# A feed-forward's gate and up projections as seven block products instead of eight, and the next block's modulation computed in another stage

## The chip, the cores and the metric

The kernel runs on one core of a Trainium2 chip. The engines are named as the profile names them: PE (TensorE, with PEld for its weight loads), DVE (VectorE), ACT (ScalarE), POOL (GpSimd) and SP (SyncE, whose queue SPq issues the loads). The metric is the device time of one execution in microseconds; lower is better.

## What is computed

Two transformer blocks over one sequence of 1024 tokens with 1024 features, all in float32. The part that the change touches, from the reference (first block, `norm_ffn`, D_FF = 2816):

```python
merged = (jax.nn.sigmoid(g_a) * (y_a @ w_branch_a[i])
          + jax.nn.sigmoid(g_b) * (y_b @ w_branch_b[i]))
x = x + merged @ w_out[i]
h = rms_norm(x, norm_ffn[i])
x = x + (jax.nn.silu(h @ w_ffn_gate[i]) * (h @ w_ffn_up[i])) @ w_ffn_down[i]
...
# second block, before anything that depends on x
mod = jax.nn.silu(c) @ w_ada[l] + b_ada[l]
sh1, sc1, g1, sh2, sc2, g2 = jnp.split(mod, 6, axis=-1)
```

`c` is one vector of 1024, `w_ada` is 1024 x 6144 (25 MB), and `mod` is wanted only after the first block's end.

## The kernel before

Activations lie transposed, feature blocks of 128 on the partitions and the 1024 tokens along the row; KD = 8 blocks of input features, KF = 22 blocks of hidden features. A float32 product is made of three passes of the type `fp32r`: an operand is cut into a high part (rounded) and a low part (the rest), and PE adds high x high, high x low and low x high. So one 128 x 128 weight block against 1024 tokens is 3 parts x 2 halves of 512 tokens = 6 matmuls, and a unit of eight blocks (`project`, L545) is 48.

Weights go through three buffers of two halves each, `w_raw`, `w_hi` and `w_lo`. The loads stand in the order of `unit_list` (L206). For every unit SP loads `w_raw` (L3387), ACT copies it to `w_hi` (L1322), and POOL subtracts the two to `w_lo` (L3092); a copy waits until PE has done with the unit two before, a load until POOL has. PE writes `psum_mem`, eight banks of 512 columns used in pairs, whose order the class `Pairs` keeps. Every engine runs its instructions in program order, and semaphores tie them to each other.

The stages around the change, in the order of time:

- gating, about 350 to 630 us: for each of eight output blocks m PE makes the gate products `ga` and `gb` (48 matmuls each) and the branch products `ba` and `bb` (24 each, weights `w_branch_a` and `w_branch_b`). DVE scales the gates by the norm (L2150), multiplies by the branch products (L2381, L2387) and adds up `merged` (L2391). For m = 0 the pooled mixer's last steps stand before it (L2329 to L2353), and the lows `ya_lo` (L2310) between.
- out, about 636 to 715 us: `w_out` times `merged`, added to x (L2400; `x1` in the code, `x_block` in the profile), whose squares are summed for the norm.
- first feed-forward, about 715 to 1460 us: ACT and DVE make `h_hi` and `h_lo` (L1549, L2145). For i = 0 to 21 PE makes gate i and up i; the norm's factor is put on behind the product (L2150, L2450), ACT applies silu, DVE multiplies by up (L2453), and ACT and DVE cut the hidden block into `hid_hi_a` and `hid_lo_a` (L1587, L2467). Two hidden blocks make a group (FFN_GROUP = 2, N_GROUPS = 11); behind the gates and ups of group g comes the down projection of group g - 1, 8 output blocks x 2 hidden blocks x 6 = 96 matmuls, added to x by DVE, one addition per output block.
- In the same stage lies the modulation: 48 loads of 512 KB on SP, three per hidden block (`modulation_steps`), on DVE 48 multiply-adds over [128 x 1024] into `ada_sum` (L2419, L2422), and on PE six times eight column sums of one column each (L819) between a gate and an up.

The helper `unscale` is L2150, `inverse` the norm's factor on ACT (L1334) and DVE (L2122), `ahead` and `unit` the filling of the weight buffers on ACT, POOL and SP.

## Time and profile before

| what | value |
|---|---|
| time, median of 3 runs | 2874.87 us (2873.45 to 2876.5) |
| span of the profiled execution | 2872.1 us |
| PE busy | 2782.7 us, 12600 matmuls |
| PEld busy | 2223.4 us |
| DVE busy | 1319.2 us, 1464 instructions |
| ACT busy | 911.8 us, 1453 instructions |
| POOL busy | 812.1 us, 436 instructions |

The profiled execution spans 2872.1 us from its first to its last instruction; the runs' median is 2.8 us more. The page has busy times and the chain that ended last; the timeline names for an instruction with idle time before it, in brackets, the engine that ended this idle time. A PE duration in the timeline is from the start of a matmul to its modelled end and overlaps the next one's, so the pace of the stream is read from the spacing of the starts. The stage tables give for a stretch each engine's busy time with the count of instructions, and PEclk, the granted TensorE clock as a share of full speed.

### The profile page before, as it was taken

How to read it: one execution, taken by the hardware profiler on the slowest of the kernel's cores; microseconds unless marked ns; L12 is line 12 of the kernel's file. 1: busy time of each engine (PE TensorE's matmuls, PEld its weight loads, DVE VectorE, ACT ScalarE, POOL GpSimd, SP SyncE). 2: the span in 40 equal slices, each digit the busy share in tenths (PEclk: the TensorE clock that was granted, in tenths of full speed). 3: DMA queues.
4: the chain of work that ended last, by engine and by line, in shares of the span. 5: the costliest groups of instructions: out<-in, count | busy, mean ns of one | idle time of the engine just before them, and what ended most of it. 6: DMA issues, size and time to landing. Idle time of an engine off the chain costs nothing.

```text
span 2872.1 us, 30939 instructions
## 1 busy us (share of the span) xinstructions
PE 2782.7 (97%) x12600; PEld 2223.4 (77%) x12600; DVE 1319.2 (46%) x1464; ACT 911.8 (32%) x1453; POOL 812.1 (28%) x436
## 2 busy tenths in 40 slices
PE   8999999999999999999999999998989999999997
PEld 6666788887788888888877677887758888888885
DVE  6777842231434334343353646436273334444446
ACT  6666521122311111111154333355353212222223
POOL 2444522224122222222244221133432222222224
PEclk9999999999999999999999999999999999999998
DMA  3000011121123222221112102132221111111113
GB/s 116 23 23 23 17 50 48 47 104 56 66 100 113 88 88 88 107 77 58 53 44 98 67 31 49 31 81 77 104 82 54 49 52 45 44 52 44 51 45 132
DMA packets 65133, 184.98 MB, mean 64 GB/s; under 512 B 6616, under 2 KB 20184, under 8 KB 64864
## 3 DMA queue, kind: packets, MB, share of 16 engines
q1 hardware_dynamic: 64992, 183.01, 18.9%
q8 instruction: 100, 1.64, 0.2%
q14 instruction: 41, 0.34, 0.0%
HBM read 167.71 MB, written 15.27 MB: 64 GB/s over the span
## 4 chain that ended last, share of the span: by engine, by line
PE 85%; DVE 5%; issue 3%; ACT 3%; POOL 2%; DMA 1%; SPq 0%; POOLq 0%; DVEq 0%; ACTq 0%
PE psum_mem L559 64%; PE psum_mem L619 2%; PE psum_mem L955 2%; PE psum_mem L960 2%; PE psum_mem L957 2%; PE psum_mem L603 2%; PE psum_mem L654 1%; PE psum_mem L709 1%; POOL w_lo L3092 1%; PE psum_mem L657 1%; PE psum_mem L655 1%; PE psum_mem L1032 1%; PE psum_mem L1297 1%; PE psum_mem L997 1%; PE psum_mem L706 1%
## 5 line engine op out<-in xcount | busy, mean ns | idle before, releaser
L3092 POOL TENSOR_TENSOR w_lo<-w_raw,w_hi 128x1024 fp32r<-128x1024 f32 (+1 forms) x233 | 548.6, 2355 | 1742.4 <-ACT w_hi L1322 1742.4
L559 PE MATMUL psum_mem<-h_hi,w_hi 128*128 128x512 f32 x2096 | 654.4, 394 | 18.8 <-ACT h_hi L1355 9.2
L559 PE MATMUL psum_mem<-h_hi,w_lo 128*128 128x512 f32 x2096 | 650.2, 392 | 8.5 <-POOL w_lo L3092 8.5
L559 PE MATMUL psum_mem<-h_lo,w_hi 128*128 128x512 f32 x2096 | 649.6, 391 | 3.6 <-DVE h_lo L2914 2.7
L559 PEld LDWEIGHTS psum_mem<-h_hi,w_hi 128*128 128x128 f32 x2096 | 394.4, 189 | 107.6 <-ACT h_hi L1355 9.2
L559 PEld LDWEIGHTS psum_mem<-h_hi,w_lo 128*128 128x128 f32 x2096 | 394.8, 189 | 94.9 <-POOL w_lo L3092 12.6
L559 PEld LDWEIGHTS psum_mem<-h_lo,w_hi 128*128 128x128 f32 x2096 | 394.5, 189 | 89.6 <-DVE h_lo L2914 3.9
L1322 ACT CAST w_hi<-w_raw 128x1024 fp32r<-128x1024 f32 (+1 forms) x233 | 234.0, 1004 | 616.1 <-PE psum_mem L559 496.7
L2150 DVE TENSOR_TENSOR tmp_mem<-psum_mem,norm_row 128x1024 f32<-128x1024 f32 x44 | 53.9, 1224 | 280.8 <-PE psum_mem L559 280.8
L2475 DVE TENSOR_TENSOR x_block<-x_block,psum_mem 128x1024 f32<-128x1024 f32 x88 | 107.3, 1220 | 68.5 <-PE psum_mem L559 65.9
L3142 POOL TENSOR_TENSOR beta<-beta,left 128x128 f32<-128x128 f32 (+2 forms) x96 | 87.7, 915 | 141.0 <-DVE left L2266 139.0
L955 PE MATMUL psum_mem<-h_hi,w_hi 128*128 128x512 f32 x272 | 113.3, 417 | 4.9 <-POOL state L3270 3.8
L2050 ACT COPY ffn_conv_in<-psum_mem 128x1024 f32<-128x1024 f32 x44 | 44.7, 1016 | 214.1 <-PE psum_mem L559 214.1
L3033 DVE TENSOR_TENSOR y_mem<-y_mem,psum_mem 128x1024 f32<-128x1024 f32 x72 | 87.9, 1220 | 52.1 <-PE psum_mem L559 49.2
L559 PE MATMUL psum_mem<-hid_lo_a,w_hi 128*128 128x512 f32 x352 | 109.7, 393 | 0.0
L559 PE MATMUL psum_mem<-hid_hi_a,w_hi 128*128 128x512 f32 x352 | 109.3, 392 | 0.0
L559 PE MATMUL psum_mem<-hid_hi_a,w_lo 128*128 128x512 f32 x352 | 108.9, 390 | 0.0
L960 PE MATMUL psum_mem<-h_hi,w_lo 128*128 128x512 f32 x272 | 107.6, 395 | 0.0
L957 PE MATMUL psum_mem<-h_lo,w_hi 128*128 128x512 f32 x272 | 107.2, 394 | 0.0
L2453 DVE TENSOR_TENSOR tmp_mem<-tmp_mem,psum_mem 128x1024 f32<-128x1024 f32 x22 | 26.9, 1221 | 166.3 <-PE psum_mem L559 166.3
L559 PE MATMUL psum_mem<-hid_hi_b,w_lo 128*128 128x512 f32 x320 | 100.9, 397 | 0.0
L559 PE MATMUL psum_mem<-hid_lo_b,w_hi 128*128 128x512 f32 x320 | 100.7, 396 | 0.0
(382 smaller groups left out, 4137.9 us busy)
## 6 DMA issues: line engine op xcount, KB each, us to landing
ada_raw<-in_w_ada SPq DMA_DIRECT2D x48, 512.0 KB, 4.8
w_raw<-in_w_up_b SPq DMA_DIRECT2D x44, 512.0 KB, 3.3
w_raw<-in_w_in_a SPq DMA_DIRECT2D x32, 512.0 KB, 3.3
w_raw<-in_w_ffn_gate SPq DMA_DIRECT2D x22, 512.0 KB, 3.6
w_raw<-in_w_ffn_up SPq DMA_DIRECT2D x22, 512.0 KB, 3.3
w_raw<-in_w_ffn_down SPq DMA_DIRECT2D x22, 512.0 KB, 4.5
w_raw<-in_w_down_b SPq DMA_DIRECT2D x22, 512.0 KB, 3.3
w_raw<-in_w_in_b_ml SPq DMA_DIRECT2D x16, 512.0 KB, 3.4
```

The lines of the kernel that those rows point to most:

```text
L559: made = e.matmul(pairs.half(use, half), wt, x[:, half_of(half)], start=at == 0 and part == 0, stop=at == len(rhs) - 1 and part == 2, skip ...
L603: made = e.matmul(pairs.half(use, half), wt, x[:, cols], start=at == 0 and part == 0, stop=at == KD - 1 and part == 2, skip_group_check=True)
L619: return e.transpose(out, in_, ident)
L955: e.matmul(bank(6 + half), high, h_hi[:, k, cols], start=k == 0, stop=False, skip_group_check=True)
L957: e.matmul(bank(6 + half), high, h_lo[:, k, cols], start=False, stop=False, skip_group_check=True)
L960: made = e.matmul(bank(6 + half), low, h_hi[:, k, cols], start=False, stop=k == KD - 1, skip_group_check=True)
L1322: e.copy(w_hi[:, i, 0:width], w_raw[:, i, 0:width]).then_inc(*S.of("w_hi", c))
L2150: return e.tensor_tensor(out, ps, row[:, :], ALU.mult)
L2475: e.tensor_tensor(x1[:, m, :], x1[:, m, :], pairs.whole(("w_down", g - 1, m)), ALU.add).then_inc(*S.of("x1", (g - 1, m)))
L3033: e.tensor_tensor(y[:, m, :], y[:, m, :], pairs.whole(("w_down2", g - 1, m)), ALU.add).then_inc(*S.of("y_add", (g - 1, m)))
L3092: e.tensor_tensor(w_lo[:, i, 0:width], w_raw[:, i, 0:width], w_hi[:, i, 0:width].bitcast(F32), ALU.subtract).then_inc(*S.of("w_lo", c))
L3142: e.tensor_tensor(kept, kept, left[i % 3][:, HALF + 1 - width:HALF + 1], ALU.mult).then_inc(*S.of("weight", i))
```

## The change

**Seven products.** A gate block i and its up block i are taken as one product of 2 x 2 blocks. The weights are U (up) and G (gate), each cut in two along the input features (low: blocks 0 to 3, high: 4 to 7); the input X is cut along features and tokens into A (low features, tokens 0 to 511), B (low, 512 to 1023), C (high, 0 to 511) and E (high, 512 to 1023). Each of the seven products has 4 blocks x 3 parts of 512 tokens, 12 matmuls. By the names of the code:

| product | weights | operand ("form") |
|---|---|---|
| UP_LOW | U low | A |
| SUM_2 | G low + G high - U low | A + E - B |
| DIFF_3 | U low - G low | E - B |
| SUM_1 | -(G low + G high) | A - B |
| UP_HIGH | U high | C |
| GATE_HIGH | G high | C - A - E + B |
| DIFF_4 | U low + U high - G low - G high | E |

The operands are made once, between the out stage and pair 0: 28 blocks of [128 x 512], each with a high part by ACT and a low part by DVE. The weight sums are made anew for each pair on DVE: `weight_low_sum` (three steps) and `weight_high_sum` (one). `w_hi` and `w_lo` are filled in four slots of [128 x 512], seven copies by ACT and seven subtractions by POOL per pair. Three products are added up in other banks' results: ACT copies products 1 and 2 and the bank of product 4 to `parts` (`part`), DVE adds `parts` to the second product's bank (`b_sum`), and the gate comes out by `gate_read`. The order of the products is the table's; in pair 0 it is SUM_2 (three blocks), UP_LOW, DIFF_3 (three blocks), the last block of both, UP_HIGH, SUM_1, GATE_HIGH, DIFF_4. PSUM keeps three banks for even and three for odd pairs. A hidden block's norm, silu and up steps are now done in halves of 512 tokens (`gate_norm`, `gate_silu`, `gate_up`). Downs stand behind pairs 2, 4, ... 18 and the last two behind pair 21.

**Modulation.** It moves from the feed-forward to the gating stage, in blocks of half the width: 96 loads of 256 KB, on DVE 96 steps of [128 x 512] (14 per output block m until they are used up, in the places that `ADA_AFTER` gives), on PE twelve times four column sums before `ga`. `c_silu` is made by ACT in the attention stage. The first two loads wait for `u_centred` 3, the end of the pooling steps on DVE, and each further load for the step two before it. The loads of `p` go to a buffer of their own instead of `tmp`.

The core of the diff, in the order PE, ACT, DVE, SP:

```diff
+UP_LOW, SUM_2, DIFF_3, SUM_1, UP_HIGH, GATE_HIGH, DIFF_4 = range(7)
...
-        mod_step = {2 + (KD * part + KD - 1) // 3: part for part in range(6)}
+        N_ADA = 6 * NH
+        ADA_AFTER = (4, 5, 3, 2)
+        def mod_in(m):
+            return [q for q in range(N_ADA) if (KD * q + KD - 1) // sum(ADA_AFTER) == m - 1]
...
+        def w_slot(mem, slot):
+            return mem[:, slot // 2, half_of(slot % 2)]
+        def w_source(j):
+            if j in (SUM_1, SUM_2):
+                return w_sums[:, 0 if j == SUM_1 else 1, :]
+            return w_raw[:, 1 if j in (DIFF_3, GATE_HIGH) else 0, half_of(j not in (UP_LOW, DIFF_3))]
+        def gu_bank(i, j):
+            return bank(7 - 3 * (i % 2) - {UP_LOW: 0, UP_HIGH: 0, SUM_2: 1, SUM_1: 1, DIFF_4: 1, DIFF_3: 2, GATE_HIGH: 2}[j])
...
+                for q in mod_in(m):
+                    modulation(q)
                 one("w_ga", ("ga", m), h_rhs("a"), (("g_a", m),))
                 one("w_gb", ("gb", m), h_rhs("a"), (("g_b", m),))
...
+            def product(i, j, blocks=range(KH)):
+                for event in {UP_LOW: (("up", (i - 2, 0)),), SUM_2: (("up", (i - 2, 1)),), DIFF_3: (("gate", (i - 2, 0)),),
+                              UP_HIGH: (("part", (i, "low")),), SUM_1: (("part", (i, "two")),),
+                              GATE_HIGH: (("gate", (i, 1)),), DIFF_4: (("part", (i, "four")),)}[j]:
+                    if i >= 2 or j > DIFF_3:
+                        w.wait_ge(*event)
+                if i == 0 and j <= DIFF_3:
+                    w.wait_ge("x1", ("out", 4 if j == DIFF_3 else 5))
+                g = down_behind(i - 1)
+                if g is not None and j in (SUM_2, DIFF_3):
+                    w.wait_ge("x1", (g, KD - 2))
+                out, slot = gu_bank(i, j), j % 4
+                for k in blocks:
+                    high, low = (w_slot(mem, slot)[:, block_of(k)] for mem in (w_hi, w_lo))
+                    for part, (wt, x) in enumerate(((high, form_hi(j, k)), (high, form_lo(j, k)), (low, form_hi(j, k)))):
+                        w.wait_ge("form_lo" if part == 1 else "form_hi", (j, k))
+                        w.wait_ge("w_lo" if part == 2 else "w_hi", ("gu", i, j))
+                        made = e.matmul(out, wt, x, start=j <= DIFF_3 and k == 0 and part == 0,
+                                        stop=k == KH - 1 and part == 2, skip_group_check=True)
+                if blocks[-1] == KH - 1:
+                    made.then_inc(*S.of("full", ("gu", i, j)))
...
+                if 0 < i < KF - 1:
+                    hidden_high(i - 1)
+                w.wait_ge("full", ("gu", i, UP_LOW))
+                if i > 0:
+                    w.wait_ge("gate", (i - 1, 1))
+                else:
+                    w.wait_ge("form", (SUM_1, KH - 1))
+                part(i, "low", 0)
+                fill_pair(i, UP_HIGH)
+                fill_pair(i, GATE_HIGH)
+                w.wait_ge("b_sum", i)
+                if i > 0:
+                    w.wait_ge("gate", (i - 1, 0))
+                part(i, "two", 1)
+                if i == 0:
+                    for k in range(KH):
+                        form_high(SUM_1, k, form_raw[:, KH + k, :])
                     out_square(KD - 1)
...
+                    w.wait_ge("form", (GATE_HIGH, KH - 1))
+                    for k in range(KH):
+                        form_high(GATE_HIGH, k, form_raw[:, k, :])
...
+                fill_pair(i, DIFF_4)
+                if i == 0:
+                    for k in range(KH):
+                        form_high(DIFF_4, k, x1[:, KH + k, half_of(1)], vec("norm_ffn", KH + k))
+                w.wait_ge("full", ("gu", i, SUM_1))
+                part(i, "four", 0)
+                if i == 0:
+                    w.wait_ge("row_v", ("ffn", 7))
+                    inverse("ffn", norm_row, tmp[:, 1, :], [bank(half) for half in range(NH)])
+                gate_silu(i, 1)
+                if down_behind(i) is not None:
+                    for slot in range(4):
+                        fill_down(down_behind(i), slot)
+                        if slot == 1:
+                            gate_silu(i, 0)
+                elif i < KF - 1:
+                    fill_pair(i + 1, UP_LOW)
+                    fill_pair(i + 1, SUM_2)
+                    gate_silu(i, 0)
+                    fill_pair(i + 1, DIFF_3)
+                    fill_pair(i + 1, SUM_1)
...
+                modulation_some(ADA_AFTER[0])
                 for b, (name, use) in enumerate((("g_a", "ga"), ("g_b", "gb"))):
                     w.own(("by_a", "merged")[b])
                     w.wait_ge("full", (use, m))
                     unscale(tmp[:, b, :], pairs.whole((use, m))).then_inc(*S.of(name, m))
+                    if b == 0:
+                        for q in mod_in(m):
+                            take_modulation(q)
+                    modulation_some(ADA_AFTER[1 + b])
...
+            def weight_low_sum(i):
+                c = ff_unit["pair", i]
+                if i > 0:
+                    w.wait_ge("w_lo", ("gu", i - 1, SUM_1))
+                w.wait_ge("in_w1", c + 1)
+                w.own("w_sum")
+                e.scalar_tensor_tensor(out=w_source(SUM_1), in0=w_source(DIFF_3), scalar=-1.0, in1=w_source(GATE_HIGH),
+                                       op0=ALU.mult, op1=ALU.subtract).then_inc(*S.of("w_sum", (i, SUM_1)))
+                w.wait_ge("in_w0", c)
+                w.own("w_sum")
+                e.tensor_tensor(w_source(DIFF_3), w_source(UP_LOW), w_source(DIFF_3),
+                                ALU.subtract).then_inc(*S.of("w_sum", (i, DIFF_3)))
+                if i > 0:
+                    w.wait_ge("w_lo", ("gu", i - 1, SUM_2))
+                e.scalar_tensor_tensor(out=w_source(SUM_2), in0=w_source(UP_LOW), scalar=-1.0, in1=w_source(SUM_1),
+                                       op0=ALU.mult, op1=ALU.subtract).then_inc(*S.of("w_sum", (i, SUM_2)))
+            def weight_high_sum(i):
+                w.wait_ge("w_lo", ("gu", i, UP_HIGH))
+                w.own("w_sum")
+                e.tensor_tensor(w_source(DIFF_4), w_source(UP_HIGH), w_source(SUM_2),
+                                ALU.subtract).then_inc(*S.of("w_sum", (i, DIFF_4)))
...
+            def gate_read(i, half):
+                s = tmp[:, i % 2, half_of(half)]
+                w.wait_ge("part", (i, "four" if half else "two"))
+                w.wait_ge("full", ("gu", i, DIFF_3 if half else GATE_HIGH))
+                e.tensor_tensor(s, parts[:, 1 - half, :], gu_bank(i, DIFF_3), ALU.add).then_inc(*S.of("gate", (i, half)))
...
+                if 0 < i < KF - 1:
+                    hidden_low(i - 1)
+                b_sum(i)
+                if i == 0:
+                    for k in range(KH):
+                        form_low(SUM_1, k, form_raw[:, KH + k, :])
                     add_square("ffn", KD - 1, norm_row[:, :], tmp[:, (KD - 2) % 2, :])
...
+                    for k in range(KH):
+                        form_low(GATE_HIGH, k, form_raw[:, k, :])
+                weight_high_sum(i)
+                if i == 0:
+                    for k in range(KH):
+                        form_low(DIFF_4, k, x1[:, KH + k, half_of(1)], vec("norm_ffn", KH + k))
+                w.own("hid_lo")
+                gate_read(i, 1)
+                if i == 0:
+                    inverse("ffn", norm_row, tmp[:, 1, :], summed_in=[bank(half) for half in range(NH)])
+                    w.own("inv_v")
+                gate_norm(i, 1, "gate_normed")
+                if down_behind(i) is None and i < KF - 1:
+                    weight_low_sum(i + 1)
+                w.wait_ge("silu", (i, 1))
+                gate_norm(i, 1, "gate_scaled")
+                gate_read(i, 0)
+                gate_norm(i, 0, "gate_normed")
+                w.wait_ge("silu", (i, 0))
+                gate_norm(i, 0, "gate_scaled")
+                gate_up(i, 0)
+                gate_up(i, 1)
...
+                    if n >= 2:
+                        w.wait_ge("ada", ((n - 2) // KD, (n - 2) % KD))
+                    else:
+                        w.wait_ge("u_centred", 3)
+                    e.dma_start(ada_raw[n % 2][:, :], io["w_ada"][q // NH, k][:, half_of(q % NH)]).then_inc(
+                        *S.of(f"in_ada{n % 2}", n, 16))
+                    yield
+            modulation = modulation_steps()
+            for m in range(KD):
+                for n in ADA_AFTER:
+                    for _ in range(n):
+                        next(modulation, None)
+                    unit()
```

Line numbers of the changed kernel are higher by about 260 on DVE and 420 on SP, so L3387 before is L3794 after.

SP's queue from the end of the attention stage on, before (`in_w_in_a` are the gate weights here, `in_w_pool` the pooled mixer's):

```order
L3387 DMA w_raw<-in_w_in_a 128x1024 x2
L3387 DMA w_raw<-in_w_pool 128x128 x2
L3387 DMA w_raw<-in_w_branch_a 128x512
L3387 DMA w_raw<-in_w_branch_b 128x512
L3387 DMA w_raw<-in_w_in_a 128x1024 x2
L3387 DMA w_raw<-in_w_branch_a 128x512
L3387 DMA w_raw<-in_w_branch_b 128x512
L3387 DMA w_raw<-in_w_in_a 128x1024 x2
L3387 DMA w_raw<-in_w_branch_a 128x512
```

The same after:

```order
L3794 DMA w_raw<-in_w_in_a 128x1024 x2
L3794 DMA w_raw<-in_w_pool 128x128
L3822 DMA ada_raw<-in_w_ada 128x512 x4
L3794 DMA w_raw<-in_w_pool 128x128
L3822 DMA ada_raw<-in_w_ada 128x512 x5
L3794 DMA w_raw<-in_w_branch_a 128x512
L3822 DMA ada_raw<-in_w_ada 128x512 x3
L3794 DMA w_raw<-in_w_branch_b 128x512
L3822 DMA ada_raw<-in_w_ada 128x512 x2
L3794 DMA w_raw<-in_w_in_a 128x1024
L3822 DMA ada_raw<-in_w_ada 128x512 x4
L3794 DMA w_raw<-in_w_in_a 128x1024
```

Nine modulation loads now stand between the gate weights and `in_w_branch_a`, three before `in_w_branch_b`, and two, four and five before the following ones.

DVE's stream at the start of the gating stage, from the last pooling step (`u_centred` 3) on, before:

```order
L2344 TENSOR_TENSOR tmp_mem<-tmp_mem,u_mem 128x16
L2353 TENSOR_TENSOR pl_lo<-tmp_mem,pl_hi 128x1024
L2150 TENSOR_TENSOR tmp_mem<-psum_mem,norm_row 128x1024 x2
L2310 SCALAR_TENSOR_TENSOR ya_lo<-psum_mem,vecs,ya_hi 128x1024 x2
L2381 TENSOR_TENSOR merged<-tmp_mem,psum_mem 128x1024
L2387 TENSOR_TENSOR tmp_mem<-tmp_mem,psum_mem 128x1024
L2391 TENSOR_TENSOR merged<-merged,tmp_mem 128x1024
```

The same after (L2635 and L2638 are the modulation's sums, L2411 the scaling of a gate, L2571 `ya_lo`, L2677 and L2684 the two branch multiplications):

```order
L2605 TENSOR_TENSOR tmp_mem<-tmp_mem,u_mem 128x16
L2614 TENSOR_TENSOR pl_lo<-tmp_mem,pl_hi 128x1024
L2635 TENSOR_SCALAR ada_sum<-ada_raw,c_silu 128x512
L2638 SCALAR_TENSOR_TENSOR ada_sum<-ada_raw,c_silu,ada_sum 128x512 x3
L2411 TENSOR_TENSOR tmp_mem<-psum_mem,norm_row 128x1024
L2638 SCALAR_TENSOR_TENSOR ada_sum<-ada_raw,c_silu,ada_sum 128x512 x4
L2635 TENSOR_SCALAR ada_sum<-ada_raw,c_silu 128x512
L2411 TENSOR_TENSOR tmp_mem<-psum_mem,norm_row 128x1024
L2638 SCALAR_TENSOR_TENSOR ada_sum<-ada_raw,c_silu,ada_sum 128x512 x3
L2571 SCALAR_TENSOR_TENSOR ya_lo<-psum_mem,vecs,ya_hi 128x1024 x2
L2677 TENSOR_TENSOR merged<-tmp_mem,psum_mem 128x1024
L2638 SCALAR_TENSOR_TENSOR ada_sum<-ada_raw,c_silu,ada_sum 128x512 x2
```

Four, five, three and two sums stand before, between and behind the gate reads, and the two `ya_lo` are behind eleven of them.

DVE's stream at the start of the first feed-forward, before, from the last addition to x on:

```order
L2400 TENSOR_TENSOR x_block<-x_block,psum_mem 128x1024
L2145 SCALAR_TENSOR_TENSOR h_lo<-x_block,vecs,h_hi 128x1024 x3
L2141 TENSOR_TENSOR norm_row<-norm_row,tmp_mem 128x1024
L2145 SCALAR_TENSOR_TENSOR h_lo<-x_block,vecs,h_hi 128x1024 x5
L2126 SCALAR_TENSOR_TENSOR tmp_mem<-psum_mem,tmp_mem 128x512
L2129 SCALAR_TENSOR_TENSOR norm_row<-tmp_mem,norm_row 128x512
L2126 SCALAR_TENSOR_TENSOR tmp_mem<-psum_mem,tmp_mem 128x512
L2129 SCALAR_TENSOR_TENSOR norm_row<-tmp_mem,norm_row 128x512
L2150 TENSOR_TENSOR tmp_mem<-psum_mem,norm_row 128x1024
L2450 TENSOR_TENSOR tmp_mem<-tmp_mem,norm_row 128x1024
L2453 TENSOR_TENSOR tmp_mem<-tmp_mem,psum_mem 128x1024
```

The same after (L2722 and L2724 make the lows of forms, L2783 is `b_sum`, L2402 a square's addition, L2715 the high weight sum, L2790 `gate_read`, L2387 the first step of the norm's factor):

```order
L2722 TENSOR_TENSOR form_lo<-form_raw,form_hi 128x512
L2724 SCALAR_TENSOR_TENSOR h_lo<-x_block,vecs,h_hi 128x512 x4
L2752 SCALAR_TENSOR_TENSOR form_raw<-x_block,vecs,form_raw 128x512
L2746 SCALAR_TENSOR_TENSOR form_raw<-x_block,vecs,parts 128x512
L2783 TENSOR_TENSOR psum_mem<-psum_mem,parts 128x512
L2722 TENSOR_TENSOR h_lo<-form_raw,h_hi 128x512 x4
L2402 TENSOR_TENSOR norm_row<-norm_row,tmp_mem 128x1024
L2722 TENSOR_TENSOR h_lo<-form_raw,h_hi 128x512 x4
L2715 TENSOR_TENSOR w_raw<-w_raw,w_sums 128x512
L2724 SCALAR_TENSOR_TENSOR h_lo<-x_block,vecs,h_hi 128x512 x4
L2790 TENSOR_TENSOR tmp_mem<-parts,psum_mem 128x512
L2387 SCALAR_TENSOR_TENSOR tmp_mem<-psum_mem,tmp_mem 128x512
```

The first `gate_read` stands behind twelve lows, a square's addition and a weight sum, all of which follow the first `b_sum`.

## Rows read from the trace of the kernel before

**Rows 1.** The page, its part 1 and its part 4 by engine.

```profile
PE 2782.7 (97%) x12600; PEld 2223.4 (77%) x12600; DVE 1319.2 (46%) x1464; ACT 911.8 (32%) x1453; POOL 812.1 (28%) x436
...
PE 85%; DVE 5%; issue 3%; ACT 3%; POOL 2%; DMA 1%; SPq 0%; POOLq 0%; DVEq 0%; ACTq 0%
```

**Rows 2.** Stretches: PE, PEld, DVE, ACT, POOL busy us (count); PEclk, DMA share, GB/s.

```profile
400.00:440.00 40.00, 40.00 (x177) 32.81 (x176) 9.45 (x6) 6.25 (x8) 8.12 (x5) 1.00 0.14 42
762.00:1455.00 693.00, 692.91 (x3090) 572.30 (x3089) 272.58 (x229) 119.27 (x117) 160.06 (x66) 1.00 0.24 85
```

**Rows 3.** Timeline of PE: start, duration, engine, line, what, idle before and releaser.

```profile
764.63 0.62 PE L559 MATMUL psum_mem<-h_hi,w_hi 128*128 128x512 f32 x2
...
799.99 0.62 PE L559 MATMUL psum_mem<-h_hi,w_hi 128*128 128x512 f32 x2
...
1700.21 0.39 PE L957 MATMUL psum_mem<-h_lo,w_hi 128*128 128x512 f32 x1
...
1702.71 0.39 PE L955 MATMUL psum_mem<-h_hi,w_hi 128*128 128x512 f32 x1
...
2826.34 0.40 PE L1297 MATMUL psum_mem<-hid_lo_b,w_hi 128*128 128x512 f32 x1
...
2829.85 0.39 PE L1297 MATMUL psum_mem<-hid_lo_b,w_hi 128*128 128x512 f32 x1
```

**Rows 4.** Groups by form: busy us, mean ns of one (last row: 760 to 1455 us).

```profile
L3092 POOL TENSOR_TENSOR w_lo<-w_raw,w_hi 128x512 fp32r<-128x512 f32 x16 | 20.7, 1296 | 127.5 <-ACT w_hi L1322 127.5
L2971 DVE SCALAR_TENSOR_TENSOR h_lo<-tmp_mem,mod,h_hi 128x512 fp32r<-128x512 f32 x16 | 12.0, 748 | 1.8 <-ACT h_hi L2003 1.4
L1322 ACT CAST w_hi<-w_raw 128x512 fp32r<-128x512 f32 x16 | 9.9, 620 | 130.2 <-PE psum_mem L559 130.2
...
L2467 DVE TENSOR_TENSOR hid_lo_a<-tmp_mem,hid_hi_a 128x1024 fp32r<-128x1024 f32 x21 | 25.6, 1220 | 3.3 <-ACT hid_hi_a L1587 3.3
```

**Rows 5.** DMA issues: count, size of one, median us from issue to landing.

```profile
w_raw<-in_w_ffn_up SPq DMA_DIRECT2D x22, 512.0 KB, 3.3
...
w_raw<-in_w_branch_a SPq DMA_DIRECT2D x8, 256.0 KB, 2.6
```

**Rows 6.** Timelines of DVE, SPq and PE, gating stage.

```profile
375.65 0.18 DVE L2344 TENSOR_TENSOR tmp_mem<-tmp_mem,u_mem 128x16 f32<-128x16 f32 x1
...
378.56 0.33 SPq L3387 DMA_DIRECT2D w_raw<-in_w_branch_a  x1
...
383.14 0.63 PE L559 MATMUL psum_mem<-ya_hi,w_hi 128*128 128x512 f32 x2
...
394.64 0.39 PE L559 MATMUL psum_mem<-h_hi,w_hi 128*128 128x512 f32 x1
...
428.92 3.33 DVE L2391 TENSOR_TENSOR merged<-merged,tmp_mem 128x1024 f32<-128x1024 f32 x1
...
461.92 3.33 DVE L2391 TENSOR_TENSOR merged<-merged,tmp_mem 128x1024 f32<-128x1024 f32 x1
```

**Rows 7.** Timelines of PE and ACT, start of the first feed-forward.

```profile
716.62 0.70 PE L559 MATMUL psum_mem<-h_hi,w_hi 128*128 128x512 f32 x2 [1.28 <-DVE x_block L2400]
...
741.28 1.04 PE L559 MATMUL psum_mem<-h_hi,w_hi 128*128 128x512 f32 x2
...
753.44 0.70 PE L559 MATMUL psum_mem<-h_hi,w_hi 128*128 128x512 f32 x2 [0.66 <-ACT w_hi L1322]
...
755.90 0.73 PE L559 MATMUL psum_mem<-h_hi,w_lo 128*128 128x512 f32 x2 [1.30 <-POOL w_lo L3092]
...
737.20 1.28 ACT L1329 ACT_TABLE_LOAD   x1
```

**Rows 8.** Timeline of POOL, gating stage.

```profile
461.79 2.39 POOL L3092 TENSOR_TENSOR w_lo<-w_raw,w_hi 128x1024 fp32r<-128x1024 f32 x1 [3.20 <-ACT w_hi L1322]
```

**Rows 9.** Timeline of PE and the table of stretches, second block.

```profile
1909.26 0.80 PE L955 MATMUL psum_mem<-h_hi,w_hi 128*128 128x512 f32 x1 [3.76 <-POOL state L3270]
...
1910.00:1919.00 9.00, 9.00 (x47) 7.73 (x46) 2.67 (x7) 3.62 (x15) 6.12 (x6) 0.76 0.31 82
```

642 lines of the change are left out of this document (431 added, 211 removed).

## The prediction

> **What bounds the kernel now.** I read the page first: TensorE (PE) is busy 97% of the span and carries 85% of the chain that ended last; the other engines are below half [rows 1]. The table by stretches then says where this matters. From 762 to 1455 us, nearly the whole first feed-forward, PE is busy 692.91 of 693.00 us at full granted clock, with DVE at 39%, POOL at 23%, ACT at 17%; a stretch of the gating stage is as full, DVE at 24%, POOL at 20% [rows 2]. So only fewer matmuls shorten either stage, and anything added costs only where PE starts to wait. The PE timeline gives the price of one: between the two rows of the gate and up stream lie 156 matmuls in 35.36 us, 0.2267 us each. The new code uses each weight block for one matmul of 512 columns, not two; a stream of that form is there already, eleven matmuls from 1700.21 to 1702.71 us, 0.2273 us each [rows 3]. I take 0.2267.
>
> **A. Fewer matmuls.** A pair (gate and up block i) was 2 x 8 x 3 x 2 = 96 matmuls and is 7 x 4 x 3 = 84, hence 22 x 12 = 264 fewer: **-59.8 us**. The down projection keeps its 96 per group, and the modulation's one-column matmuls (96 rows) only move: 0.
>
> **B. Does a steady pair stay at PE's pace?** A pair is now 84 x 0.2267 = 19.04 us, a product 2.72. Durations of the new 512-wide steps, from their nearest rows: ACT copy 0.62, DVE 0.75, POOL low half 1.30 [rows 4]. Per pair that is DVE 13 x 0.75 + 1.22 = 11.0 us, POOL 7 x 1.30 = 9.1, ACT 12 x 0.62 and one of at most twice that = 8.7: none is a bound. The waits, in order, from the end of pair i: DVE's last multiply ends 1.6 us in, then ACT's hidden high part (1.2), its copy of the first product (0.62), DVE's hidden low part (1.22), until 4.7 us. The second product ends at 5.44; add on DVE, copy on ACT: 6.9 us. The fourth product may start at 8.16: 1.2 us to spare. Later: copy of the fourth product, then DVE's read, ready 1.5 us after it, before the sixth product at 2.72: again 1.2. Weights for the next pair: a raw half leaves after POOL's last low half, lands 3.3 us later [rows 5], and is split 2 to 3 us before use. I cost the steady pairs at **0**; if this cover goes, rival 2 has the price. In the down groups DVE has 2.75 us per block for one addition of 1.22, and the three weight sums (2.2 us) stand behind the fourth: late by less than one block, 0.
>
> **C. Modulation in the gating stage, first block.** The order printed above puts the nine first modulation loads ahead of `w_branch_a` on SP, all behind the last pool step on DVE, at 375.83 us; before, that load left at 378.56 [rows 6]. There are two buffers, so two loads go per round of load (2.6, the row of the same size, rows 5), sum (0.75) and the signals: 3.5 us. Loads 0 and 1 land at 378.6, sums 2 and 3 end at 383.4, then the gate read (1.2), sums 6 and 7 at 390; load 8, then `w_branch_a` leaves at 390.0, lands at 392.6, is cast 0.6 and subtracted 1.3 later. PE wanted it at 383.14 [rows 6]. DVE also makes `ya_lo` 2 and 3 behind sum 11, at 400.6, which that product needs for its last two blocks. Branch b then ends at 407.3, against 394.6 before, where the next block's first matmul starts [rows 6]: **+12.7**.
>
> **D. The other blocks.** A block took 33.0 us: the additions at 428.92 and 461.92 [rows 6]. Fourteen sums are seven rounds, 25 us, but broken by the four reads. Worst is `w_branch_b`: it leaves after sum 9, which stands behind the second gate read, at 24.6 us into the block, lands with its neighbour's traffic at 27.9, is cast at 28.6 and has its low half at 30.0; PE wants it at 27.6 and 28.5. I take 1.5 us for each of six blocks (the next block's cast is late by less), **+9**. The bounds are 0 (load alone at 2.6, a little PE time from the moved matmuls) and 3.5 (every load of the block late).
>
> **E. The first pair.** Before, pair 1 began 26.0 us after the start and lost 0.66 + 1.30 in its second unit [rows 7]. Now DVE forms 4 x 7 operand blocks and their low halves. Counted from the end of the last out block, T (715.3, one wait of 1.28 ahead of the row at 716.62): DVE reaches the last forms at T+13.5, because 4 lows, and form 4 and 1 of block 3, stand ahead of the copy the fifth product waits for; that product's weights are there at T+16, PE having run out at T+10. Sixth product: its bank is freed by a read that stands on DVE behind 4 + 1 + 4 + 1 + 4 steps (order above), T+30, PE having run out at T+21. Then the sum, ACT's two table loads (1.28 each, rows 7) and six inverse steps of half a row (0.62) stand ahead of the weight cast of pair 1: T+41, PE having run out at T+36.4. Pair 1 is effectively under way at T+42.6 and loses 0.9 more at its fourth product. Before, the same point was at 26.0 + 1.96 = T+28.0; with the 2.7 us that A already books, **+18**. Bounds: 8 (half of these waits overlap) and 28 (POOL's halves come in between, next paragraph).
>
> What POOL can do to DVE a row shows: DVE's `merged` started at 461.92 beside POOL's `w_lo` of 461.79 to 464.18 and took 3.33 us, where the same form beside nothing takes 1.22 [rows 4, 6, 8]. The Trainium skill, SBUF — State Buffer, Who interferes with whom, says that a DVE instruction with two SBUF inputs and a GpSimd instruction that reads SBUF exclude each other for a whole instruction, and the trace agrees. By that rule every weight sum, norm multiplication and low half here competes with POOL; that is rival 2.
>
> **F. The clock.** Around a PE wait of 3.76 us the granted clock is 0.76 over 9 us: 0.24 x 9 = 2.2 us lost against full speed, the mean of a stretch at 2.4 GHz and one at the lower level, 1.2 GHz [rows 9]. C and E bring four waits of 4 us and more: 4 x 2.2 = **+9**; bounds 0 and 15. The Trainium skill, TensorE: Matmul & The Clock Gate, What's actually happening, says the gate passes half the pulses after idleness; the row agrees.
>
> **Sum.** -59.8 + 12.7 + 9 + 18 + 9 = -11. The end of the stage keeps its steps in their order (last additions, squares, sum): 0. The profiled execution spans 2872.1 us, the runs' median is 2874.87, 2.8 more: 2861 of span, **2864 us**.
>
> **The rivals.** (1) *The starts hide better*: C at 7, D 0, E 8, F 2, a gain of 43, **2832 us**. For: ACT and DVE have over half their time free in both stages; my chains add every step end to end. Against: the SP and DVE orders are strict. (2) *DVE and POOL block each other in every pair* (slower): POOL holds 9.1 us of a pair, DVE's eight steps with two SBUF inputs and the hidden low part 6.8, together 15.9 of 19.04. If two halves of 1.3 us fall into the chain of B, 2.6 less the 1.2 to spare is 1.4 us per pair, 21 pairs: +29, **2893 us**. It decides the sign from 11 / 21 = 0.5 us per pair. For: that load. Against: POOL's halves in B fall mostly where DVE waits for PE, and all DVE steps on a PSUM bank (the b sum, reads, up) have one SBUF input and no row shows them held up. (3) *The new stream is slower*: at the 0.234 us per matmul of the last down block (15 from 2826.34 to 2829.85, rows 3), 22 x 84 x 0.0073 adds 13 us: **2877 us**, no change. Against: the rows at 1700.21 and 1702.71, whose operands are `h_hi` as here. (4) *The change doesn't act*, the stage being bound by weight loads: 2875 or more; PE's full windows and PEld at 83% speak against it, I give it nothing.
>
> **How the numbers follow.** Measurement tells about 0.2%, 5.7 us, so "faster" is below 2869. Forecast 0.50 (0.39 faster, 0.09 same, 0.02 slower, as its bounds lie), rival 1 0.25, rival 2 0.14, rival 3 0.11 (0.01 faster, 0.06 same, 0.04 slower). Faster 0.65, same 0.15, slower 0.20. The range runs from just past rival 1 to just short of rival 2: 2828 to 2888.
>
> **What would show it.** Right: the pair matmuls' count down by 264 at 0.227 us; PE full from pair 2 on, about 627 us for the stage without its start; PE waits before `w_branch_a` near 384 us (about 9 us) and before every `w_branch_b`; in the first pair waits for DVE's `tmp_mem` read and ACT's `w_hi`; several short dips of the clock. Wrong: PE gaps in each pair before the fourth or sixth product, released by DVE or POOL (rival 2); no gap at `w_branch_a` (C false).

## The result and the profile after

The changed kernel takes **2899.76 us** (median of 4 runs, 2897.57 to 2906.73) against 2875.68 for the kernel before in the same comparison (4 runs): a ratio of 1.0088 with a 95% interval of 1.0071 to 1.0105. It is slower by 24 us, where 2864 with a range of 2828 to 2888 was predicted. The profiled execution spans 2895.8 us, 23.7 more than the one before. Times are medians of all runs; in the comparisons below one run of the kernel before and one of the third-buffer kernel took over 4500 us, and the ratios leave such slow runs out.

The page, its part 1 and its part 4 by engine, which answer to [rows 1]:

```profile
PE 2758.6 (95%) x12336; PEld 2185.1 (75%) x12336; DVE 1499.7 (52%) x1774; ACT 1015.9 (35%) x1698; POOL 925.9 (32%) x568
...
PE 79%; DVE 7%; issue 6%; ACT 3%; POOL 3%; DMA 2%; SPq 0%; DVEq 0%; POOLq 0%; ACTq 0%
```

The 264 matmuls are gone (12600 to 12336), but PE's share fell from 97% to 95%: PE stands idle 48 us longer than before (137.2 us against 89.4). The table of stretches of the changed kernel says where. It shows the end of gating block 0, the blocks 1, 2, 3 and 6 and the steady part of the feed-forward (columns as in [rows 2]):

```profile
378.00:412.00 34.00, 22.45 (x78) 16.87 (x77) 19.81 (x20) 8.44 (x11) 6.73 (x5) 0.75 0.44 142
412.00:448.00 36.00, 34.84 (x155) 27.76 (x154) 12.04 (x15) 4.22 (x5) 4.97 (x3) 1.00 0.36 117
448.00:495.00 47.00, 38.61 (x160) 30.64 (x159) 20.62 (x24) 6.32 (x7) 8.26 (x5) 0.85 0.40 134
495.00:536.00 41.00, 37.40 (x161) 29.63 (x160) 20.23 (x23) 5.26 (x6) 7.73 (x5) 0.96 0.44 141
...
608.00:654.00 46.00, 37.76 (x165) 30.12 (x164) 20.70 (x25) 6.41 (x8) 9.93 (x5) 0.89 0.45 141
...
824.00:1430.00 606.00, 606.00 (x2620) 491.76 (x2619) 323.69 (x362) 190.23 (x307) 252.90 (x183) 1.00 0.16 53
```

The steady feed-forward is full, as forecast. The gating blocks 1 to 7, 33.0 us each before, are not alike: 35.9, 47.3, 41.0, 36.2, 35.4, 45.8 and 34.8 us, and block 0 ends 18 us late. By the starts of the PE rows the stages compare so:

| stage | before, us | after, us | difference |
|---|---|---|---|
| up to the end of gating block 0 | 394.40 | 412.12 | +17.7 |
| gating blocks 1 to 7 | 231.0 | 276.3 | +45.3 |
| out stage | 89.9 | 88.9 | -1.0 |
| first feed-forward, to the sum of its squares | 753.8 | 719.2 | -34.5 |
| the rest | 1403.0 | 1399.2 | -3.8 |

The last row is the second block, which the change leaves as it was; the profiles of the other kernels with the same second block have 1403 to 1406 us there, and why this one has 1399 is not known. So the feed-forward gave 34.5 us and the gating stage took 63.0. PE's longest waits, summed over the run (the page of waits: engine and line, releaser, us in total, times, longest):

```profile
PE psum_mem L652 <- ACT w_hi L1482: 30.2, 12, 7.9
PE psum_mem L652 <- POOL w_lo L3479: 10.3, 10, 1.5
...
PE psum_mem L936 <- ACT w_hi L1711: 7.7, 2, 3.9
PE psum_mem L964 <- DVE x_block L2816: 7.2, 4, 4.3
PE psum_mem L936 <- DVE tmp_mem L2790: 6.0, 1, 6.0
```

Of the first line 29.3 us, in 11 waits, lie in the gating stage. What ends such a wait, at the start of block 2, is seen when the timelines of DVE, SPq and PE are laid side by side:

```profile
436.92 0.74 DVE L2638 SCALAR_TENSOR_TENSOR ada_sum<-ada_raw,c_silu,ada_sum 128x512 f32<-128x512 f32 x1
449.05 0.49 DVE L2635 TENSOR_SCALAR ada_sum<-ada_raw,c_silu 128x512 f32<-128x512 f32 x1 [11.40 <-PE psum_mem L881]
...
438.11 0.38 SPq L3794 DMA_DIRECT2D w_raw<-in_w_branch_b  x1
449.57 1.18 SPq L3822 DMA_DIRECT2D ada_raw<-in_w_ada  x2
450.85 0.38 SPq L3794 DMA_DIRECT2D w_raw<-in_w_in_a  x1
...
448.00 1.84 PE L881 MATMUL psum_mem<-consts,ada_sum 128*128 128x1 f32 x16
456.73 1.19 PE L652 MATMUL psum_mem<-h_hi,w_hi 128*128 128x512 f32 x2 [6.89 <-ACT w_hi L1482]
```

A modulation unit is one of the twelve blocks of 512 columns, numbered from 0. DVE is through with unit 2 at 437.7 and stands **11.40 us**, because unit 3 writes the same one of the two `ada_sum` buffers as unit 1, and PE makes unit 1's column sums only at the start of the next block (L881, 448.00). SP's next modulation loads wait for DVE's sums, and behind them in its queue stands the gate weight of block 2 (L3794 at 450.85). It leaves 2.9 us after PE began the block that needs it. The label on PE's wait is ACT, four links behind the cause. The same happens where unit 10 begins, at block 6: DVE stands 11.42 us and PE then waits 6.87.

### The profile page after: what moved, and what is told of

It is laid out like the page before. It is cut to its first block, busy times and chain, and to the rows that moved or that the text cites. A ratio compares the mean times of both kernels' runs of the same rounds, so it can differ in the third digit from the quotient of the medians.

```text
span 2895.8 us, 31514 instructions
## 1 busy us (share of the span) xinstructions
PE 2758.6 (95%) x12336; PEld 2185.1 (75%) x12336; DVE 1499.7 (52%) x1774; ACT 1015.9 (35%) x1698; POOL 925.9 (32%) x568
## 4 chain that ended last, share of the span: by engine, by line
PE 79%; DVE 7%; issue 6%; ACT 3%; POOL 3%; DMA 2%; SPq 0%; DVEq 0%; POOLq 0%; ACTq 0%
PE psum_mem L652 36%; PE psum_mem L936 14%; PE psum_mem L964 8%; PE psum_mem L712 2%; PE psum_mem L1115 2%; PE psum_mem L1120 2%; PE psum_mem L1117 2%; POOL w_lo L3479 2%; PE psum_mem L696 1%; PE psum_mem L747 1%; PE psum_mem L802 1%; PE psum_mem L750 1%; PE psum_mem L748 1%; DMA ada_raw<-in_w_ada 1%; PE psum_mem L1192 1%
## 5 line engine op out<-in xcount | busy, mean ns | idle before, releaser
L3479 POOL TENSOR_TENSOR w_lo<-w_raw,w_hi 128x1024 fp32r<-128x1024 f32 (+2 forms) x167 | 386.8, 2316 | 1232.1 <-ACT w_hi L1482 1219.5
L652 PE MATMUL psum_mem<-h_hi,w_hi 128*128 128x512 f32 x1392 | 440.0, 398 | 29.4 <-ACT w_hi L1482 16.0
L652 PE MATMUL psum_mem<-h_hi,w_lo 128*128 128x512 f32 x1392 | 434.9, 394 | 9.1 <-POOL w_lo L3479 9.1
L652 PEld LDWEIGHTS psum_mem<-h_hi,w_hi 128*128 128x128 f32 x1392 | 263.7, 191 | 90.1 <-DVE tmp_mem L2684 13.9
L1482 ACT CAST w_hi<-w_raw 128x1024 fp32r<-128x1024 f32 (+2 forms) x167 | 165.2, 989 | 450.3 <-PE psum_mem L652 194.7
L652 PEld LDWEIGHTS psum_mem<-h_hi,w_lo 128*128 128x128 f32 x1392 | 263.3, 190 | 69.5 <-POOL w_lo L3479 14.7
L652 PEld LDWEIGHTS psum_mem<-h_lo,w_hi 128*128 128x128 f32 x1392 | 264.9, 191 | 61.3 <-DVE h_lo L3301 3.6
L3571 POOL TENSOR_TENSOR w_lo<-w_raw,w_hi 128x512 fp32r<-128x512 f32 x154 | 216.6, 1410 | 294.4 <-ACT w_hi L1711 294.2
L2816 DVE TENSOR_TENSOR x_block<-x_block,psum_mem 128x1024 f32<-128x1024 f32 x88 | 107.4, 1221 | 101.6 <-PE psum_mem L964 101.4
L1711 ACT CAST w_hi<-w_raw 128x512 fp32r<-128x512 f32 x154 | 94.7, 622 | 167.0 <-PE psum_mem L936 81.9
L936 PE MATMUL psum_mem<-h_hi,w_lo 128*128 128x512 f32 x352 | 138.8, 394 | 0.1
L936 PE MATMUL psum_mem<-form_hi,w_hi 128*128 128x512 f32 x264 | 105.6, 400 | 3.7 <-ACT w_hi L1711 3.7
L1120 PE MATMUL psum_mem<-h_hi,w_lo 128*128 128x512 f32 x272 | 107.4, 395 | 0.0
L936 PE MATMUL psum_mem<-form_hi,w_lo 128*128 128x512 f32 x264 | 105.7, 401 | 1.5 <-POOL w_lo L3571 1.5
```

The costliest lines, as they stand in the source:

```text
L652: made = e.matmul(pairs.half(use, half), wt, x[:, half_of(half)], start=at == 0 and part == 0, stop=at == len(rhs) - 1 and part == 2, skip ...
L936: made = e.matmul(out, wt, x, start=j <= DIFF_3 and k == 0 and part == 0, stop=k == KH - 1 and part == 2, skip_group_check=True)
L1120: made = e.matmul(bank(6 + half), low, h_hi[:, k, cols], start=False, stop=k == KD - 1, skip_group_check=True)
L1482: e.copy(w_hi[:, i, 0:width], w_raw[:, i, 0:width]).then_inc(*S.of("w_hi", c))
L1711: e.copy(w_slot(w_hi, slot), source).then_inc(*S.of("w_hi", key))
L2816: e.tensor_tensor(x1[:, m, :], x1[:, m, :], down_banks(g, m), ALU.add).then_inc(*S.of("x1", (g, m)))
```

## The experiments

Every comparison is with the kernel before, run on the same chip in between (its medians were 2876.1 to 2876.8 us). A number in the text that is not a median comes from the profile of that run.

### The modulation left out, after and before

In both kernels the loads of `w_ada`, the weighted sums and the column sums are left out, so `mod` is only `b_ada`. The core of the edit, in the changed kernel:

```diff
-                for q in mod_in(m):
-                    modulation(q)
...
-                w.wait_ge("full", ("mod", q))
-                e.tensor_tensor(mod[:, cols], pairs.whole(("mod", q))[:, 0:KH], vec("b_ada", q * KH, KH),
-                                ALU.add).then_inc(*S.of("mod", q))
+                e.tensor_scalar(mod[:, cols], vec("b_ada", q * KH, KH), 1.0, None, ALU.mult).then_inc(*S.of("mod", q))
```

> The changed kernel with the modulation left out: no loads of w_ada, no weighted sums, no column sums; mod is only b_ada. Theory 1 (the loss lies in how the modulation is interleaved with the gating stage): the gating stage falls back from 318 us to about 255 us, the time to about 2836 (2899.8 less 63). Rival (the seven products themselves are no gain, the gating stage is slow for another reason, such as the three new halves' pace): 2875 or more.

> The kernel before with the modulation left out in the same way. Its 96 column sums take 0.106 us each in the trace, so both theories expect 2875.7 - 10 = 2865. The difference to after_no_mod is what the seven products alone are worth: 29 us by theory 1 (59.8 less the first pair 17, the end 7 and a slower pace 8), under 10 us by the rival. If it were 2850 or less, the modulation had cost more than its column sums before, too.

Measured: 2844.02 us after (ratio 0.9876, 0.9861 to 0.9890) and 2866.48 before (0.9958, 0.9943 to 0.9973). The gating blocks are 33.0 us each in both. The kernel after is 8 us above the 2836 that theory 1 expected. So the seven products alone are worth 22.5 us, not 29, and the modulation costs 55.7 us in the changed kernel and 9.8 in the one before. The last number is about its column sums: 96 rows of 0.106 us each in the trace, 10.2 us. The loss is in the interleaving, as theory 1 has it; the seven products are a gain, though 7 us smaller than stated.

### A third buffer for the weighted sums

```diff
+        third_sum = merged[:, KD - 1, HALF:T]
+        sums = [ada_sum[0][:, :], ada_sum[1][:, :], third_sum]
...
-                            if q > 1:
-                                w.wait_ge("full", ("mod", q - 2))
+                            if q > 2:
+                                w.wait_ge("full", ("mod", q - 3))
```

> The changed kernel with a third buffer for the weighted sums (it lies in the last row of merged, unused until block 7), so that the first sum of unit q waits for the column sums of q - 3, not q - 2. Theory 1a (the long waits come from DVE standing 11.4 us for column sums that PE has only at the start of the next block, with the weight loads queued behind): the two waits of 6.9 us at blocks 2 and 6 and the 1.4 + 1.2 of block 3 go, with their clock loss 25 to 33 us: 2868 to 2875. Rival 1b (the weight loads are late because they stand behind the modulation's loads on SP, two buffers being too few for them, whatever DVE waits for): the waits stay, less than 8 us is gained.

Measured: 2877.92 us (0.9998, 0.9986 to 1.0010), 21.8 less than the change and just above the 2868 to 2875 expected. The gating stage ends 27.3 us earlier (661.15 instead of 688.43). Of that, 2.4 arose in block 0, where the edit does not act yet; 24.9 are blocks 1 to 7, which all take 35 to 36.5 us, and the timeline of DVE and SPq at the same place reads:

```profile
435.12 0.48 DVE L2637 TENSOR_SCALAR ada_sum<-ada_raw,c_silu 128x512 f32<-128x512 f32 x1
...
439.27 0.38 SPq L3796 DMA_DIRECT2D w_raw<-in_w_in_a  x1
```

DVE goes on without a wait and the gate weight leaves at 439.27, 6 us ahead of block 2. Both 6.9 us waits and the two at the start of block 3 are gone. Rival 1b (two load buffers are too few, whatever DVE waits for) is out: their number was not touched. The total gained 5.5 us less than the stage; in the two profiles the second block, the same in both kernels, took 1404.8 us here and 1399.2 with the change.

### The weight loads ahead of the modulation loads

```diff
                 for n in ADA_AFTER:
+                    unit()
                     for _ in range(n):
                         next(modulation, None)
-                    unit()
```

> The changed kernel with only SP's order turned round: in each place the weight load first, then the modulation loads. DVE still stands for the column sums. Theory 1a and 1b both expect the waits for w_hi to go, since no weight load is behind a modulation load of its own place: first block 17.7 to about 5 us of loss, blocks 2 and 6 from 14 to about 4 each, 30 to 40 us gained in all: 2860 to 2870. If DVE's wait holds PE up by itself (reads of the gates and branches late, banks not free), less than 20 us is gained.

Measured: 2878.25 us (1.0005, 0.9995 to 1.0014), 21.5 less than the change, where both theories expected 30 to 40: at the edge of the case in which DVE's wait holds PE up by itself. Blocks 3, 4 and 7 now take 34.8 us and blocks 1 and 5 33.9, which is 33.0 and two or one sets of column sums (0.85 us each): nothing else is left of the modulation there. Blocks 2 and 6 take 39.2 and 39.6, with this row at the start of block 2:

```profile
450.91 1.22 PE L652 MATMUL psum_mem<-h_hi,w_hi 128*128 128x512 f32 x2 [1.74 <-DVE merged L2677]
```

PE waits for a bank that DVE, still standing for the column sums, reads late. The wait is only 1.74 us, but the granted clock is 0.50 around it (451 to 455 us), and the slower matmuls cost 2.8 more. And the first block is no better than before the edit (+19.0 us), with another label:

```profile
402.84 1.22 PE L652 MATMUL psum_mem<-ya_lo,w_hi 128*128 128x512 f32 x2 [13.79 <-DVE ya_lo L2571]
```

There the twelve sums that stand ahead of `ya_lo` on DVE hold PE up by themselves, and the late weight mattered little beside them. Term C of the prediction had both paths, and its end, 407.3, was reckoned from `ya_lo`; the expectation of this run (17.7 to about 5 us) had left that path out.

### The gating stage mended

The third buffer, the loads first, and no sum ahead of the first block's gate reads and `ya_lo`:

```diff
+        def ada_after(m):
+            return (0, 0, 6, 8) if m == 0 else ADA_AFTER
...
-                    modulation_some(ADA_AFTER[1 + b])
-                if m == 0:
-                    map_low(2)
-                    map_low(3)
+                    if m == 0 and b == 1:
+                        map_low(2)
+                        map_low(3)
+                    modulation_some(ada_after(m)[1 + b])
```

> The changed kernel with the third buffer for the sums, the weight loads ahead of the modulation loads on SP, and in the first block no sum ahead of the gate reads and ya_lo (0, 0, 6, 8 instead of 4, 5, 3, 2). If theory 1a is whole, nothing but the column sums (0.106 us each, 10 us in all) is left of the modulation in this stage: gating 266 to 272 us instead of 318, out stage from 2 us behind 625.4 + 10, the time 2844 + 10 = 2854 to 2862. If DMA traffic or DVE's and POOL's sharing cost by themselves, blocks stay above 34.5 us each and the time above 2868.

Measured: 2862.76 us (0.9953, 0.9938 to 0.9968), just above what was expected, and 0.5% less than the kernel before. The stage ends 23.4 us behind that of before, not 63.0. Two of its blocks in the table of stretches:

```profile
475.80:510.60 34.80, 34.80 (x161) 28.80 (x160) 20.28 (x22) 5.46 (x6) 7.50 (x4) 1.00 0.48 151
510.60:545.40 34.80, 34.80 (x162) 28.82 (x161) 18.96 (x22) 5.47 (x6) 6.86 (x4) 1.00 0.44 145
```

DVE is busy 20 of 35 us and the DMA moves over three times what it did in [rows 2], and PE waits for nothing in them. Neither the traffic nor the sharing between DVE and POOL costs anything here. What stays is a wait of 5.9 us ahead of block 1's column sums, for the eighth sum, since none starts before the lows. Block 1 then takes 38.1 us, its first 6 at a granted clock near 0.50, and block 2 36.3, with one wait of 1.2 us for `w_lo`.

### Thirty-two bytes of padding

The prediction gave 0.11 to a slower stream (rival 3), and the timeline of the changed kernel shows it: pairs 3 and 4 with the down group between them and the next pair.

```profile
883.42 0.39 PE L936 MATMUL psum_mem<-form_hi,w_hi 128*128 128x512 f32 x1
...
922.06 0.63 PE L964 MATMUL psum_mem<-hid_hi_a,w_hi 128*128 128x512 f32 x2
...
944.46 0.39 PE L936 MATMUL psum_mem<-form_hi,w_hi 128*128 128x512 f32 x1
```

Two pairs take 38.64 us, 0.2300 per matmul, and a down group 22.40, 0.2333 (before 21.99). Within a pair the three products on `form_*` go at 0.2333, the four on `h_*` at 0.2267. Before the change too, matmuls on `ya_*`, `yb_*` and `hid_*_b` were at 0.2333. The buffers of the fast kind begin, in each partition, at the same address modulo 256 as the weights: `w_hi` begins at byte 28384 and `h_hi` at 57056, both 224 modulo 256, but `form_hi` at 155392 and `hid_hi_a` at 204544, both 0, which is 32 off. In the kernel before `hid_hi_a` was 64 off and `hid_hi_b` 96. Two kernels add unused bytes:

```diff
         eps_col = sb("eps_col", [P, 2])
+        sb("pad", [P, 8])
```

> The changed kernel with 32 unused bytes per partition behind the buffers that live all through (a pad of 8 floats). Before it, weights and h_hi/h_lo begin at an address 32 past a multiple of 64 in each partition, and form_hi, form_lo, hid_*_a, ya, yb at a multiple of 64; the pad moves the second kind to 32 past, like the first. In the trace matmuls on h_* start 0.2267 us apart, on form_* and hid_* 0.2333. Theory 2 (the pace hangs on where the streamed operand lies): form_* and hid_*_a fall to 0.2267, a pair from 19.32 to 19.04 us, a down group from 22.40 to 21.76, the feed-forward by 6 + 7 = 13 us, ya and yb by 2.6, and hid_*_b too, 6: 2899.8 - 20 = 2880. Rival (the pace belongs to something else of these streams, such as one bank per weight load or the halves' readers): no change, 2900.

> The kernel before with the same 32 bytes ahead of the weight buffers: now weights, h_* and hid_*_a lie at multiples of 64, ya, yb, hid_*_b at 32 past. Theory 2a (what counts is the streamed operand's own address): h_* slows down to 0.2333, ya, yb and hid_*_b come to 0.2267; 7000 matmuls x 0.0067 = 47 us more and some 8 us less: 2915. Theory 2b (what counts is that operand and weights lie alike): h_* stays at 0.2267, yb and hid_*_b (32 against 0) stay at 0.2333: 2876. Rival (no address matters): every pace as before.

Measured for the pad behind the common buffers: 2895.90 us (1.0065, 1.0048 to 1.0081), 3.9 less than the change; the feed-forward is 7.3 us shorter, the second block, 1404.4 us in this profile, 5.2 longer. The same places:

```profile
884.33 0.39 PE L937 MATMUL psum_mem<-form_hi,w_hi 128*128 128x512 f32 x1
...
922.69 0.63 PE L965 MATMUL psum_mem<-hid_hi_a,w_hi 128*128 128x512 f32 x2
...
944.68 0.39 PE L937 MATMUL psum_mem<-form_hi,w_hi 128*128 128x512 f32 x1
```

38.36 and 21.99: `form_*` and `hid_*_a`, now 64 off, go at 0.229, two thirds of the way. `hid_*_b`, now 128 off, stayed at 0.2334. So the address counts, but the expected 0.2267 was wrong. With the pad ahead of the weights in the kernel before the time was 2876.41 (1.0000, 0.9990 to 1.0011): this pad moves the weights and every buffer behind them by 32 bytes, so that their addresses change and no distance between them does. `h_*` kept 0.2267 and `yb_*` 0.2333. That rejects 2a (the operand's own address) and leaves the distance between operand and weights.

### Pair 0 in another order

The edit orders the small steps of pair 0 as the expectation says; in its core, on DVE:

```diff
                 weight_high_sum(i)
-                if i == 0:
-                    for k in range(KH):
-                        form_low(DIFF_4, k, x1[:, KH + k, half_of(1)], vec("norm_ffn", KH + k))
                 w.own("hid_lo")
                 gate_read(i, 1)
                 if i == 0:
+                    for k in range(KH):
+                        form_low(DIFF_4, k, x1[:, KH + k, half_of(1)], vec("norm_ffn", KH + k))
+                    gate_read(0, 0)
+                    weight_low_sum(1)
                     inverse("ffn", norm_row, tmp[:, 1, :], summed_in=[bank(half) for half in range(NH)])
```

> The changed kernel with pair 0 alone in another order: ACT fills UP_HIGH's and GATE_HIGH's weights ahead of its first copy, DVE makes the first gate_read ahead of DIFF_4's lows and the second ahead of the norm's factor, PE sums the squares ahead of GATE_HIGH, pair 1's first two weight slots are filled before and amid ACT's steps for the factor, hidden block 0 is cut after pair 1's b_sum. Theory 3 (the 15 us of waits in the first pair are the order of the small steps, nothing else): the wait of 6.0 us for the read and that of 3.8 for w_hi all but go, pair 1 starts 28 to 31 us after the stage's start instead of 40.7, and may lose up to 3 us in its middle: 8 to 12 us less, 2888 to 2892. Rival (ACT and DVE are simply full there, so any order moves the wait): under 3 us gained.

Measured: 2892.54 us (1.0058, 1.0041 to 1.0075), 7.2 less than the change and just short of the 8 to 12 expected; the feed-forward is 9.1 us shorter. The changed kernel's waits in the first pair were

```profile
790.57 0.77 PE L936 MATMUL psum_mem<-h_hi,w_hi 128*128 128x512 f32 x1 [3.95 <-ACT w_hi L1711]
...
804.84 0.79 PE L936 MATMUL psum_mem<-h_hi,w_hi 128*128 128x512 f32 x1 [6.04 <-DVE tmp_mem L2790]
...
818.03 0.50 PE L936 MATMUL psum_mem<-form_hi,w_hi 128*128 128x512 f32 x1 [3.75 <-ACT w_hi L1711]
819.98 0.79 PE L936 MATMUL psum_mem<-form_hi,w_lo 128*128 128x512 f32 x1 [1.22 <-POOL w_lo L3571]
```

and in the reordered one

```profile
794.22 0.79 PE L936 MATMUL psum_mem<-h_hi,w_hi 128*128 128x512 f32 x1 [5.32 <-ACT parts L1776]
...
804.73 0.50 PE L936 MATMUL psum_mem<-h_hi,w_hi 128*128 128x512 f32 x1 [0.69 <-DVE tmp_mem L2801]
```

The wait for the read fell from 6.04 to 0.69 and pair 1 starts at 810.3, 30.7 us into the stage instead of 40.7. That of 3.75 for `w_hi` fell to 1.60, but 1.4 us in two waits for `w_lo` came in pair 1. The first wait did not go: SUM_1 cannot start before ACT's copy, which DVE's last form releases. As I read it, that is the amount of work between the out stage and pair 0 and not its order; no run here took it apart. The rival (any order only moves the wait, under 3 us gained) is out.

### All together

Gating mended, pair 0 reordered, two hidden lows behind the first additions of a down group, and 224 unused bytes ahead of `form_hi`:

```diff
+        sb_in(ff1, "pad", [P, 56])
         form_hi_mem = sb_in(ff1, "form_hi", [P, 3, KH, HALF], F32R)
...
-            for i in range(HID_LAST, KF):
-                hidden_low(i)
             for m in range(KD):
                 down_add(N_GROUPS - 2, m)
+                if m in (1, 2):
+                    hidden_low(HID_LAST + m - 1)
```

> Gating mended (2862.8 measured), pair 0 reordered, the last two hidden lows behind the first additions of down group 9, and 224 unused bytes ahead of form_hi, so that form_* and hid_*_a lie at the same offset within 256 bytes as the weights and h_*. If the pace of a stream hangs on that offset, a pair comes from 19.32 to 19.04 us and a down group from 22.40 to 21.76 or less, 13 us; if 64 bytes are what counts, 19.18 and 21.99 as with the pad of 32, 7 us. Sum: 2862.8 - 10 (first pair) - 2 (end) - 7 to 13: 2838 to 2844, faster than both kernels by over 1%. Rival: the gains overlap (the stage's end or the DVE steps take them back) and it stays above 2852.

Measured: **2841.39 us** (0.9884, 0.9868 to 0.9901). The pace, at the pairs of the same kind:

```profile
893.80 0.39 PE L942 MATMUL psum_mem<-form_hi,w_hi 128*128 128x512 f32 x1
...
931.88 0.62 PE L970 MATMUL psum_mem<-hid_hi_a,w_hi 128*128 128x512 f32 x2
...
953.64 0.39 PE L942 MATMUL psum_mem<-form_hi,w_hi 128*128 128x512 f32 x1
```

Two pairs 38.08 and a down group 21.76, both exactly 0.2267 per matmul. The two hidden lows were worth little: one wait of 1.2 us at the stage's end went, the one of 4.3 stayed. The section on the prediction shows what that one hangs on.

The last two kernels carry the addresses through: the kernel before with nothing but unused bytes, and the mended one with the same bytes for the second block.

```diff
+            sb_in(ff, "pad_b", [P, 40])
             hid_hi_b = [sb_in(ff, f"hid_hi_b{i}", [P, FFN_GROUP, T], F32R) for i in range(2)]
```

> The kernel before with nothing but unused bytes: ahead of p_*, of hid_*_a and of hid_*_b, so that all three lie at the same offset within 256 bytes as the weights. Theory 2c (a matmul starts 0.2267 us after the last where streamed operand and weights lie alike within 256 bytes, 0.229 where they differ by 64, 0.2334 otherwise): the second block's down groups from 22.4 to 21.8 us, 1056 x 0.0067 = 7 us, the first block's from 21.99 to 21.76, 2.5 us: 2876.5 - 9.5 = 2867. Rival (it holds for the form_* stream only): 2874 or more.

> all_mended (2841.4) with the same bytes ahead of p_*, hid_*_last and hid_*_b, and in the first block's gating 0, 2, 6, 6 sums instead of 0, 0, 6, 8, so that the first column sums don't wait. Theory 2c: 7 to 8 us less in the second block; the wait of 5.4 us at block 1 falls to 2 or less and its clock loss with it, 3 to 5 us: 2829 to 2832. Rival: above 2838.

Measured: 2866.46 us (0.9961, 0.9949 to 0.9972) for the kernel before with the bytes, 10.2 less for no instruction changed, and **2833.66 us** (0.9849, 0.9836 to 0.9862) for the best version, 43 less than the kernel before. A down group of the second block in the former:

```profile
2535.36 0.61 PE L562 MATMUL psum_mem<-hid_hi_b,w_hi 128*128 128x512 f32 x2
...
2557.12 0.62 PE L562 MATMUL psum_mem<-h_hi,w_hi 128*128 128x512 f32 x2
```

21.76 us, where the kernel before has 22.41:

```profile
2537.95 0.63 PE L559 MATMUL psum_mem<-hid_hi_b,w_hi 128*128 128x512 f32 x2
...
2560.36 0.63 PE L559 MATMUL psum_mem<-h_hi,w_hi 128*128 128x512 f32 x2
```

The other edit of the best version, 0, 2, 6, 6 sums in block 0, missed: the wait fell from 5.4 to 3.1 us, but the gating stage ended at 648.3 as in the version ahead of it.

## Why the prediction was wrong

**A** held: 264 matmuls fewer, and at the pace of `h_*` 59.8 us. **B** held too: from 824 to 1430 us PE is busy 606.00 of 606.00 us, and rival 2 (DVE and POOL block each other) did not come, although POOL's half-width step took 1.41 us on average with 42% load. The time lies near rival 2's 2893, but not for its reason.

**D was the step that failed.** It priced the blocks behind the first at 9 us (1.5 for each of six, with a bound of 3.5), and blocks 1 to 7 took 45.3: 22.3 of waits, 10.2 of column sums and 12.8 more, most of them slower matmuls (see F). The step that it called the worst, `w_branch_b`, cost less than it said: six waits of 0.6 to 0.9 us, 4.4 in all. The one that it dismissed, "the next block's cast is late by less", cost 6.89 us at block 2 and 6.87 at block 6. The term walked through DVE's sums and SP's loads block by block and asked when each load leaves. It did not ask what the sums themselves wait for. The kernel's line on the wait for the column sums of q - 2 is in the part that moved, and in the feed-forward it never bound. With two buffers, 8 sums per unit and 14 per block, units 3, 5 and 10 begin before PE has reached the column sums that they need, and DVE stands 11.40, 6.54 and 11.42 us there, 29.4 in all. The run with the third buffer shows what that is worth: 24.9 us in these blocks. The 10.2 us of column sums moved here from the feed-forward, where they went out of the sum again: the 0 for them was right.

**C** was forecast as +12.7 and was +16.3 (17.7, of which 1.4 arose ahead of the stage). Both waits that it named came, for `w_branch_a` and for `ya_lo`:

```profile
395.36 1.19 PE L652 MATMUL psum_mem<-ya_hi,w_hi 128*128 128x512 f32 x2 [7.91 <-ACT w_hi L1482]
...
402.54 0.98 PE L652 MATMUL psum_mem<-ya_lo,w_hi 128*128 128x512 f32 x2 [1.83 <-DVE ya_lo L2571]
```

The predicted 9 us wait before `w_branch_a` was 7.91. One of 1.81 us for the second pool weight, behind four modulation loads, was not foreseen, and 4.8 us of the 16.3 are matmuls at the lower clock.

**E** was right in its end: pair 1 under way 42.6 us after the start was forecast, 41.9 measured (818.03, 1.22 more, less 777.35), with the waits for `w_hi`, the read and `w_hi` at their places. They were shorter than forecast (3.95, 6.04 and 3.75 us for about 6, 9 and 5), and the 0.9 us more at its fourth product did not come. The slower matmuls between these waits are in the 41.9.

**F** was mis-sized and in the wrong place. It gave four waits 2.2 us each, three of them in the first pair. In the gating stage PE's waits sum to 33.8 us, the column sums to 10.2, 1.4 came from ahead, and 63.0 less these leaves 17.6 us. Of these, 14.9 lie in blocks 0, 2, 3 and 6, where the granted clock is 0.75, 0.85, 0.96 and 0.89, and are put down to matmuls at the lower clock; the other 2.7 are spread over blocks whose clock is 1.00, and their cause is open. The blocks with a wait of about 7 us lost 3.0 and 4.3 more than their waits, and with the loads first the blocks with one of 1.7 us, right behind the column sums, lost 2.8 and 3.1 more.

**The end of the stage**, costed at 0 because its steps keep their order, took 7.2 us in four waits for DVE's additions (L2816). The last down groups follow pair 21 at once, and on DVE the lows of its hidden blocks stand ahead of the additions: that is the wait of 1.21. Two in the last group, 0.30 and 1.37, were not looked into. The one of 4.33 hangs on another step that moved, the low part of `p`:

```profile
1442.57 0.62 ACT L1711 CAST w_hi<-w_raw 128x512 fp32r<-128x512 f32 x1 [6.39 <-PE psum_mem L964]
1443.10 1.99 ACT L1850 CAST p_hi<-p_raw 128x1024 fp32r<-128x1024 f32 x2
...
1444.17 1.51 DVE L2862 TENSOR_TENSOR p_lo<-p_raw,p_hi 128x1024 fp32r<-128x1024 f32 x1 [6.22 <-ACT p_hi L1850]
...
1446.87 0.85 PE L964 MATMUL psum_mem<-hid_hi_a,w_hi 128*128 128x512 f32 x2 [4.33 <-DVE x_block L2816]
```

ACT makes `p_hi` behind a weight copy that waits for PE, DVE makes `p_lo` ahead of its third addition, and PE waits for that addition. Before, `p_lo` was made ahead of the last two groups' additions (L2462). No run here takes this apart; that the wait stayed at 4.33 when the hidden lows were moved fits it.

**The pace** (rival 3, 13 us at 0.234 in all seven products) was half right: three of seven products go at 0.2333, 5.6 us, and the down groups, which it left out, add 4.5. The row at 2826.34 that it came from was an instance of the same effect, and "whose operands are `h_hi` as here" overlooked that three products read `form_*`.

In all: -59.8, then +63.0 for the gating stage less the 10.2 of column sums that the feed-forward gave up, +16.6 for the first pair (13.9 and the 2.7 that A books), +7.2 and +10.1 give +26.9; the out stage and the rest were 4.8 us shorter, which gives 22.1, and the span is 23.7 longer. The 1.6 left over was not taken apart in full: beyond their pace and their waits, pairs 1 and 2 took 3.1 us more (the first pairs before 1.0) and the last two down groups 2.6, while a wait before the sum of the squares fell from 2.52 to 0.88.

## What to carry to other kernels

When work is moved to another place, list every wait of the moved code again, those that never bound included, and for each ask where the releasing step now stands in its own engine's order; the two buffers of the weighted sums never held anything up in the feed-forward and became a stall where PE took the sums only at the start of a block. On a queue that issues in order, as SP's does here, put the loads that the bound engine needs ahead of those that serve side work, since everything behind a waiting load waits with it; with that order alone the late-weight waits of the gating stage, 29.3 us, were gone. And before a matmul stream is called full, compare its pace by operand: a spacing of 0.233 instead of 0.227 us shows as 100% busy and was worth 10 us here for a few unused bytes.

## What the runs showed of the hardware

A 128x512 matmul in fp32r starts 0.2267 us after the last when the streamed operand and the weights begin at the same address modulo 256 in the partition, 0.229 when they differ by 64, and 0.2334 when they differ by 32 (either way), 96 or 128 bytes; other distances were not tried. Moving both together changes nothing (the kernel before with the pad ahead of its weights). All of it is at the full granted clock with PE shown as busy throughout. What in the chip makes this is not shown by these runs.

DVE at 20 of 35 us, POOL at 7 and a DMA share of 0.48 (151 GB/s) beside a full PE stream cost PE nothing (the mended gating blocks: 33.0 us and the column sums). A column sum, a float32 matmul of one column, shows as two rows of 0.106 us each, so that it costs about as much as one fp32r matmul of 512 columns.

In the changed kernel the granted clock falls to 0.50, the lower level of 1.2 GHz, in or right behind PE's long waits (6.89 us before 456.73, 6.04 before 804.84, 3.75 before 818.03) and is back at 1.00 at 464, 809 and 826 us, each time after PE had worked on at the lower clock. There a matmul of 512 columns starts 0.427 us after the last.
